# Re-timing how a Strassen product chain changes its resident operand, in the fp32 tail of a hybrid transformer block

## The reference

```python
x_lat = x_lat + m_lat[2] * y_lat                      # y_lat = concat([ya, yb]) @ w_out
h_lat = modulate(rms_norm(x_lat, norm2_g[l]), m_lat[3], m_lat[4])
x_lat = x_lat + m_lat[5] * jnp.square(jax.nn.relu(h_lat @ w1)) @ w2   # w1 1024x4096, w2 4096x1024
return rms_norm(x_lat, final_g)
```

## Time and profile before

| | |
|---|---|
| median of 3 runs | 3885.58 us (3885.14 to 3890.12) |
| profiled execution, own time | 3882.01 us |
| its span, first to last instruction | 3880.2 us |
| last stage (`phase_out`), first to last product | 2408.3 to about 3868 us |
| one undisturbed unit, 84 matmuls | 19.0 us |
| mean granted TensorE clock over the span | 0.923 |

### The profile page before, as it was taken

How to read it: one execution, slowest core, us unless ns; L and a number is a source line. 1 busy time by engine, 2 the same in 40 slices (tenths; PEclk the granted TensorE clock), 3 DMA queues, 4 the chain that set the end, 5 groups by cost and what they waited for, 6 DMA issues and landing times. The chain is left out here.

```text
span 3880.2 us, 98954 instructions
## 1 busy us (share of the span) xinstructions
PE 3376.9 (87%) x41449; PEld 2794.3 (72%) x41449; DVE 1982.7 (51%) x2884; ACT 1644.7 (42%) x2375; POOL 1675.8 (43%) x1364
## 2 busy tenths in 40 slices
PE   6899999999878888867777653999999999999998
PEld 3677888888767777756767523877887887877877
DVE  5588401110045555554455556575556556567575
ACT  5566314432145555532333412564455444323243
POOL 0220223222045545524555324545655665565564
PEclk8999999999989999996677766999999999999999
DMA  5133434453233333325343345566565557646453
GB/s 194 47 76 73 99 90 137 123 138 99 83 101 105 111 103 106 107 89 111 83 101 88 133 157 190 194 235 194 194 232 195 179 199 264 224 174 238 174 217 120
DMA packets 438927, 560.19 MB, mean 144 GB/s; under 512 B 119852, under 2 KB 355728, under 8 KB 413720
## 3 DMA queue, kind: packets, MB, share of 16 engines
q1 hardware_dynamic: 412704, 518.84, 42.1%
q10 hardware_dynamic: 20344, 21.04, 1.7%
q0 software_dynamic: 5632, 16.78, 1.5%
HBM read 354.42 MB, written 202.16 MB: 143 GB/s over the span
## 5 line engine op out<-in xcount | busy, mean ns | idle before, releaser
L2814 PE MATMUL o_pg<-o_t_hi,o_s_hi 128*128 128x512 f32 x2016 | 794.5, 394 | 60.7 <-DVE o_part L2992 18.5
L2816 PE MATMUL o_pg<-o_t_lo,o_s_hi 128*128 128x512 f32 x2016 | 790.7, 392 | 0.0
L2817 PE MATMUL o_pg<-o_t_hi,o_s_lo 128*128 128x512 f32 x2016 | 790.3, 392 | 0.0
L601 PE MATMUL p_pg<-h_hi,p_whi 128*128 128x512 f32 (+1 forms) x1384 | 530.8, 384 | 9.6 <-DVE p_wlo L830 9.6
L601 PE MATMUL p_pg<-h_hi,p_wlo 128*128 128x512 f32 (+1 forms) x1384 | 518.7, 375 | 0.0
L601 PE MATMUL p_pg<-h_lo,p_whi 128*128 128x512 f32 (+1 forms) x1384 | 518.6, 375 | 0.0
L2814 PEld LDWEIGHTS o_pg<-o_t_hi,o_s_hi 128*128 128x128 f32 x2016 | 382.2, 190 | 150.2 <-issue 38.1
L2817 PEld LDWEIGHTS o_pg<-o_t_hi,o_s_lo 128*128 128x128 f32 x2016 | 382.2, 190 | 79.9
L2816 PEld LDWEIGHTS o_pg<-o_t_lo,o_s_hi 128*128 128x128 f32 x2016 | 382.6, 190 | 79.2
L3011 DVE TENSOR_TENSOR o_s_lo<-o_raw,o_s_hi 128x512 fp32r<-128x512 f32 x288 | 263.1, 914 | 204.3 <-ACT o_s_hi L2850 204.1
L601 PEld LDWEIGHTS p_pg<-h_hi,p_whi 128*128 128x128 f32 x1384 | 261.8, 189 | 60.9 <-DVE p_wlo L830 9.8
(11 more groups left out here) (333 smaller groups left out, 6641.0 us busy)
## 6 DMA issues: line engine op xcount, KB each, us to landing
o_raw<-in_w_mlp SPq DMA_DIRECT2D x32, 1024.0 KB, 5.9
scr_f<-o_xf SPq DMA_DIRECT2D x64, 512.0 KB, 7.7
o_raw<-scr_f SPq DMA_DIRECT2D x32, 1024.0 KB, 5.4
scr_w<-o_pre SPq DMA_DIRECT2D x16, 1792.0 KB, 6.7
o_t_raw<-scr_w SPq DMA_DIRECT2D x28, 1024.0 KB, 5.5
g_kqvb<-scr_kqv SPq DMA_DIRECT2D x72, 384.0 KB, 3.5
o_xf<-scr_x SPq DMA_DIRECT2D x22, 1024.0 KB, 8.4
p_raw<-in_w_in SPq DMA_DIRECT2D x38, 512.0 KB, 5.9
```

The costliest lines, as they stand in the source:

```text
L601: last = nc.tensor.matmul(pg[0:m, bank, 0:n], w[:, q, k, 0:m], h[bank][:, k, :], start=(k == 0 and j == 0), stop=(k == KT - 1 and j == 2))
L2814: nc.tensor.matmul(out, s_hi[:, q, k, :], t_hi[:, q, k, :], start=(not more and k == 0), stop=False, skip_group_check=more)
L2816: nc.tensor.matmul(out, s_hi[:, q, k, :], t_lo[:, q, k, :], start=False, stop=False, skip_group_check=more)
L2817: last = nc.tensor.matmul(out, s_lo[:, q, k, :], t_hi[:, q, k, :], start=False, stop=(k == 3), skip_group_check=more)
```

## The change

It alters only orders and slots; no arithmetic, no semaphore and no buffer is added or removed.

- **T's low parts.** `T_LOW` lists slots counted from the last unit's slot 0. Parts 0 to 3 stay in slots 3 to 6; part 4 moves from slot 7 (first unit, q=0) to 8, part 5 from 8 to 9, part 6 from 9 to 10. On VectorE `t_low` now stands ahead of the slot's `s_low`.
- **T's high parts** keep their slots (2 to 8). On ScalarE `t_high` and the slot's `s_high` now stand ahead of `f_unit` for q > 2.
- **Second unit's S parts.** Before: slots 3, 4, 5, 6 of the first unit make parts 0; 1, 2; 3, 4; 5, 6. After: slots 4, 5, 6 make 0; 1, 2; 3, 4, and slot 0 of the second unit makes 5, 6 and then part 0 of the third.
- **Loads.** The second unit's `raw_load` moves from last unit slot 5 (ahead of T's parts 5 and 6) to first unit slot 0 (behind all of T); the third unit's moves from first unit slot 1 to slot 2, behind the store of slot 1.
- **Mixed sums on GpSimd.** The second unit's move from slots 1 to 3 of the first unit to its slot 4, behind the `x_add` of slot 4. The third unit's move from slots 5 and 6 of the first unit and slot 0 of the second, all to slot 0 of the second.

```diff
-T_HIGH, T_LOW = 2, 3
-LATE_PREP = ((), (), (), (0,), (1, 2), (3, 4), (5, 6))
+T_HIGH = (2, 3, 4, 5, 6, 7, 8)
+T_LOW = (3, 4, 5, 6, 8, 9, 10)
+LATE_PREP = {4: (0,), 5: (1, 2), 6: (3, 4), 7: (5, 6)}
...
             if i - 1 in LAST_OF:
-                return [(i + 1, p) for p in LATE_PREP[q]]
-            return [(i + 1, q)] if i + 1 < N else []
+                return [(i + 1, p) for p in LATE_PREP.get(q, ())]
+            late = [(i, p) for p in LATE_PREP.get(q + 7, ())] if i - 2 in LAST_OF else []
+            return late + ([(i + 1, q)] if i + 1 < N else [])
...
-        def exchange(i, q, lag):
-
-            at = 7 * i + q - lag
-            i, q = divmod(at, 7)
-            return (LAST_OF[i], q) if i in LAST_OF else None
+        def exchange(i, q, at):
+
+            for last in (i, i - 1):
+                if last in LAST_OF and 7 * (i - last) + q in at:
+                    return LAST_OF[last], at.index(7 * (i - last) + q)
+            return None
...   SyncE
-                        if q == (5 if last else 1 if first else 0) and i + 2 < N:
+                        if first and q == 0:
+                            raw_load(i + 1)
+                        if q == (2 if first else 0) and i + 2 < N and not last:
                             raw_load(i + 2)
...   GpSimd
-                        if q == 0 and 1 <= i + 1 < N and i >= 0 and i - 1 not in LAST_OF:
+                        if q == 0 and 1 <= i + 1 < N and i >= 0 and i - 1 not in LAST_OF and i - 2 not in LAST_OF:
                             mix_end(i + 1)
...
-                        if q == 5 and i + 2 < N and i not in LAST_OF:
+                        if q == 5 and i + 2 < N and i not in LAST_OF and i - 1 not in LAST_OF:
                             mix_start(i + 2)
-                        if q == 6 and i + 2 < N and i not in LAST_OF:
+                        if q == 6 and i + 2 < N and i not in LAST_OF and i - 1 not in LAST_OF:
                             mix_turn(i + 2)
-                        if i - 1 in LAST_OF:
-                            if q == 1:
-                                mix_start(i + 1)
-                            if q == 2:
-                                mix_turn(i + 1)
-                            if q == 3:
-                                mix_end(i + 1)
+                        if i - 1 in LAST_OF and q == 4:
+                            mix_start(i + 1)
+                            mix_turn(i + 1)
+                            mix_end(i + 1)
+                        if i - 2 in LAST_OF and q == 0:
+                            mix_start(i + 1)
+                            mix_turn(i + 1)
+                            mix_end(i + 1)
...   ScalarE
-                            if not is_x(i):
+                            if not is_x(i) and q == 2:
                                 f_unit(i, q)
-                        for at in prepared(i, q):
-                            s_high(*at)
                         if exchange(i, q, T_HIGH):
                             t_high(*exchange(i, q, T_HIGH))
+                            for at in prepared(i, q):
+                                s_high(*at)
+                        if 0 <= i < N and not is_x(i) and q > 2:
+                            f_unit(i, q)
+                        if not exchange(i, q, T_HIGH):
+                            for at in prepared(i, q):
+                                s_high(*at)
...   VectorE
+                        if exchange(i, q, T_LOW):
+                            t_low(*exchange(i, q, T_LOW))
                         for at in prepared(i, q):
                             s_low(*at)
-                        if exchange(i, q, T_LOW):
-                            t_low(*exchange(i, q, T_LOW))
```

## The result

The changed kernel took 3892.64 us, median of 20 runs (3884.20 to 3907.22), beside 3884.32 us before, also of 20. One of the 20 runs before took 6099.54 us and stands outside the ratio. The ratio is 1.003, 95% interval 1.0019 to 1.0040: slower by about 0.3%, some 12 us; the medians are 8.3 us apart. The forecast was 3887.4 with a change of +1.8 us. The time lies in the range and the loss has the forecast's sign, but it is some six times the forecast's, and to a loss beyond 0.2% I had given 0.19.

The account below looks back on a forecast made before the run. TensorE was busy 87% of the span, with about 64 us of exchange excess as the ceiling; +3.3 + 0.6 + 2.1 - 4.2 = +1.8 on the profiled 3882.0, plus 3.6 to the median, gave 3887.4 us, range 3861 to 3900.

Parts of the forecast that it names:

- X exchange, first unit: Units 48, 56, 64: product 3 idles only 1.6 us for its combine, clock stays up; unit 48 gains 5.6 us.
- X exchange, second unit: Units 49, 57, 65: product 3 waits 4.2 us, clock costs 2.1; 6.9 us lost each, three exchanges +3.3.
- (a): Rival: the second unit of an exchange waits, but the clock stays up; 3875.7 us, chance 0.20.
- (b): Rival: the second unit hardly waits, as VectorE fits its `s_low` into GpSimd's pauses; 3855 us, chance 0.15.
- Exchange at 40: F to X: unit 40 ends 2.7 us earlier, unit 41's idle grows from 1.51 to about 4.2, clock falls; +2.1.
- Exchange at 24: F to F: `take_p1` 1.7 us earlier, unit 24 -2.6; unit 25's product 3 waits 3.3; +0.6 in sum.
- Exchange at 8: X to F: unit 9 loses 0.5 and 2.5 us, shorter `take_h` wait returns 2.7 and 4.5; -4.2.
- Rival (c): Slower: the second unit's sums come later still, and each slip passes whole to products 1 and 3; 3898 us, chance 0.15.

Follow-up runs that it names:

- e8: Changed kernel with four kinds of GpSimd operation at 8 columns in place of 512, results incomplete; last stage 1439.8 us against 1460.0 before, no ratio.
- e1: Kernel before with only VectorE's part of the change (low parts 4 to 6 one slot later, ahead of the slot's `s_low`); ratio 0.9968 to the kernel before.
- e3: Changed kernel with the second unit's GpSimd sums back in slots 1 to 3 and raw loads where they were; ratio 0.9985 to the kernel before.
- e5: Changed kernel with the store of h issued ahead of unit 11's raw load in slot 0 of unit 9; ratio 1.0018 to the kernel before.
- e4: Kernel before with only ScalarE's new order, `t_high` and `s_high` ahead of `f_unit`; ratio 1.0014 to the kernel before.
- e11: Kernel before, executed again without an edit; last stage 1457.2 us against 1460.0 in the first trace, no ratio.

## Why the forecast was right or wrong

- **X exchange, first unit: right.** 21.0 forecast, 21.0 measured, with 1.46 us of wait against 1.6.
- **X exchange, second unit: right in mechanism and size.** Product 1's wait 0.5 (0.38), the combine at 12.1 us (12.2), product 3's wait 4.2 (6.86 from product 2 in place of 2.72, with 3.98 idle), the clock's price 2.1: 2.5 in unit 49, 1.7 in 57 and 65. Forecast +3.3 for the three pairs, measured +3.1. e8 shows that the turns with GpSimd are the cause and not the number of parts; e1 and e3 that the sums' new place brings them about. Rivals (a) and (b) fall.
- **Exchange at 40: right.** +2.1 forecast; unit 40 -3.9 (-2.7 forecast), unit 41 +4.9, and 0.7 in unit 39: about +1.6. The pair took 50.4 here and 51.7 in e5, with the same streams there, against 49.4 in both traces of before. Product 3 of unit 41 waited 4.33 us, 4.2 forecast, and the clock fell.
- **Exchange at 24: small in sum, as forecast, but both terms were too small.** -4.5 and +5.0 in place of -2.6 and +3.2. ScalarE kept the pace of 3.52 that I had read; the rows of the changed kernel that answer to the earlier trace rows:

```profile
2918.58 1.92 ACT L2860 ACTIVATE o_t_hi<-o_t_raw 128x2048 fp32r<-128x2048 f32 x1 [2.76 <-DMA o_t_raw<-scr_h]
...
2924.43 0.62 ACT L2879 ACTIVATE o_xf<-o_xf 128x512 f32<-128x512 f32 x1
...
2927.94 0.61 ACT L2879 ACTIVATE o_xf<-o_xf 128x512 f32<-128x512 f32 x1
...
2929.12 0.58 ACT L2867 ACTIVATE o_part<-o_pg 128x512 f32<-128x512 f32 x1
```

  From `t_high` 2 to `take_p1` it took 10.5 us, 10.6 forecast. But `t_high` 2 started 2.3 us ahead of unit 24's first product and not 1.0, partly because unit 23 had grown by 0.7. So the first unit's wait was 3.35 and not 4.7, and the clock cost 1.5 less there than before; the forecast's -2.6 held 0.9 beyond the 1.7 of `take_p1`, for which I gave no term. Unit 25's wait was 3.23, 3.3 forecast, and the clock cost 1.6 and not half of 1.7.
- **Exchange at 8: the step that failed.** I forecast -4.2 and units 7 to 23 came out 4.3 longer. Three things.

  First, the gains behind unit 9's product 3. Counted from unit 8's start, product 3 of unit 9 was to start 0.5 later and to cost 2.5 by the clock; it started 1.6 earlier, as unit 8 gave 3.9 and not 2.6, and cost 2.4 (5.25 in place of 2.84). The two gains behind it are what failed: -2.7 at product 6 of unit 9 came out as -0.1 (it still waited 2.38 us), and -4.5 in unit 10 as -0.6. I had reasoned that the joined h pieces are done earlier and `take_h` no longer waits as long; that looked at VectorE and not at SyncE's stream. `take_h` waited 10.89 us in place of 7.21: the store stood behind a raw load that waits for `s_low(9,6)`, the very part that the change had moved later. 4.3 us, by e5, where the store goes out 30.7 us after unit 8's start, against 34.5 in the changed kernel and 35.8 before: the pieces were ready 5.1 us earlier (4 forecast), of which the store kept 1.3. With e5's swap the wait at product 6 of unit 9 went whole, 2.8 us gained there on the kernel before, but of the 4.5 in unit 10 only 1.9 came.

  Second, unit 7 lost 2.3 by ScalarE's order, which e4 shows alone, and unit 23 lost 0.7 by the same order. Third, the rest, 0.9, is in units 12 to 15; e11, which has no edit, has 0.5 more there than the first trace of before, so most of it may be spread.
- **The sum.** All but the exchange at 8: +6.0 forecast, +5.2 measured. With it: +1.8 against +9.5. The forecast was of this small size because a gain of 4.2 stood against losses of 6.0, and that gain didn't come. That the time still lies in the range is owed to the range, 39 us wide. Rival (c) has the sign and nearly the size, but its mechanism, sums that slip further, didn't occur.

## What to carry to other kernels

When a stall is cured by moving work later, write down every stream that waits for the moved instruction, the DMA-issuing one first: a load that waits at the head of an in-order queue holds the stores behind it, and those hold another engine. Two engines that take turns at a port should be given their work in different stretches; a queue of short operations behind a late producer costs more than twice its own time. And a kernel whose parts each help at some places and hurt at others is best cut by place: all edits everywhere gave 1.003; with ScalarE's order, the second unit's late sums and the raw loads left out, and the rest only where it paid, it was 0.995.

## What the runs showed of the hardware

- The clock's price isn't fixed by the wait. Most waits repeat to a few hundredths, yet unit 49 lost 2.5 us after 3.98 idle and units 57 and 65 1.7 after the same; in e11 the same 4.8 us wait cost 1.5 where it had cost 2.5. Product 3 of unit 9 took 2.84 after 1.99 idle in the kernel before, and 4.42 after 1.97 in e11. In unit 7, 0.5 to 0.7 us more of wait turned 3.84 us of transposes into 5.47.
- The order of arrival decides who pays where VectorE and GpSimd meet: with `t_low` first it takes 2.27 and GpSimd's `x_add` 3.27; with the `x_add` first that takes 1.69 and `t_low` 3.40. Where both have a queue, both pay: 3.33 a `t_low` and 3.32 a sum.
- The stages ahead of an unaltered point start it anywhere within 19 us from one execution to the next. An effect of 3 us is plain in the lengths of the X units and lost in the total of one trace; at 24 and 40 single traces with the same streams differ by up to 2.4 us in a unit.
